# Mixture-of-experts stage: experts in order of their tokens, with rows by place and weights fetched by register

## What is computed

```python
def route(h2, w_router, router_bias):      # h2: (1088, 1024); 64 experts, each token takes 8
    s = sigmoid(h2 @ w_router); sb = s + router_bias
    ...                                     # best 4 of 8 groups by their two best scores, then top 8 of them
    w = s[idx] / sum(s[idx]) * 2.5
def routed_experts(h2, idx, wts, w_gate, w_up, w_down):
    xb = h2[toks]                           # tokens of expert e
    hb = silu(xb @ w_gate[e]) * (xb @ w_up[e])      # 1024 -> 256
    y = y.at[toks].add((hb @ w_down[e]) * ws[:, None])   # 256 -> 1024
```

## Time and profile before

| | us |
|---|---|
| median of 3 runs (2910.75 to 2916.51) | 2913.45 |
| the profiled execution | 2915.86 |
| its span, first to last instruction | 2914.1 |

### The profile page before, as it was taken

How to read it: one execution, slowest core, us unless ns; L and a number is a source line. 1 busy time by engine, 2 the same in 40 slices (tenths; PEclk the granted TensorE clock), 3 DMA queues, 4 the chain that set the end, 5 groups by cost and what they waited for, 6 DMA issues and landing times. The chain is left out here.

```text
span 2914.1 us, 43099 instructions
## 1 busy us (share of the span) xinstructions
PE 2641.9 (91%) x15610; PEld 2333.5 (80%) x15610; DVE 1934.3 (66%) x3001; ACT 1288.1 (44%) x1831; POOL 1491.7 (51%) x1668
## 2 busy tenths in 40 slices
PE   5999899898998989989869995999999999999991
PEld 5789698896978969789667654888888888888880
DVE  6474756647566475664776873777777777777764
ACT  3423424235252342523432312656666666666552
POOL 6455655646556465664652652454545444454530
PEclk9999999999999999999989997999999999999995
DMA  5101011110111101111034217899999999999966
GB/s 169 53 23 56 24 37 41 31 56 24 37 41 31 56 24 37 41 31 55 16 120 146 73 32 213 259 273 280 274 282 269 272 281 282 273 272 278 274 171 220
DMA packets 309592, 395.36 MB, mean 136 GB/s; under 512 B 22226, under 2 KB 260114, under 8 KB 309458
## 3 DMA queue, kind: packets, MB, share of 16 engines
q1 hardware_dynamic: 277250, 303.05, 31.9%
q0 software_dynamic: 30976, 86.09, 12.3%
q10 hardware_dynamic: 1232, 4.46, 0.6%
HBM read 324.15 MB, written 84.07 MB: 140 GB/s over the span
## 5 line engine op out<-in xcount | busy, mean ns | idle before, releaser
L113 PE MATMUL ps<-xTh,w_mix_low 128*128 128x368 f32 (+1 forms) x1728 | 594.2, 344 | 1.4 <-DVE xTl L107 1.4
L114 PE MATMUL ps<-xTl,w_mix_high 128*128 128x368 f32 (+1 forms) x1728 | 570.7, 330 | 0.0
L115 PE MATMUL ps<-xTh,w_mix_high 128*128 128x368 f32 (+1 forms) x1728 | 569.1, 329 | 0.0
L113 PEld LDWEIGHTS ps<-xTh,w_mix_low 128*128 128x128 f32 x1728 | 327.5, 190 | 10.6 <-issue 8.7
L114 PEld LDWEIGHTS ps<-xTl,w_mix_high 128*128 128x128 f32 x1728 | 327.6, 190 | 8.4 <-issue 7.0
L115 PEld LDWEIGHTS ps<-xTh,w_mix_high 128*128 128x128 f32 x1728 | 326.8, 189 | 0.0
L2028 PE MATMUL ps<-xghl,wgh 128*128 128x384 f32 x1024 | 298.9, 361 | 7.1 <-DVE xghl L107 7.1
L2028 PE MATMUL ps<-xghl,wuh 128*128 128x384 f32 x1024 | 296.1, 359 | 0.0
L1971 POOL DMA_INDIRECT ys_d<-yo,back x128 | 254.1, 1985 | 76.4 <-POOL back L1967 48.3
L2030 PE MATMUL ps<-xghl,wgl 128*128 128x192 f32 x1024 | 258.2, 252 | 0.0
L2030 PE MATMUL ps<-xghl,wul 128*128 128x192 f32 x1024 | 256.6, 251 | 0.0
(11 more groups left out here) (348 smaller groups left out, 6217.6 us busy)
## 6 DMA issues: line engine op xcount, KB each, us to landing
wg<-in_w_exp_gate SPq DMA_DIRECT2D x64, 1024.0 KB, 8.5
wu<-in_w_exp_up SPq DMA_DIRECT2D x64, 1024.0 KB
wd<-in_w_exp_down SPq DMA_DIRECT2D x64, 1024.0 KB
w_mix_raw<-in_w_in SPq DMA_DIRECT2D x72, 512.0 KB, 3.8
mT_d<-gs_m SPq DMA_DIRECT2D x8, 544.0 KB, 2.7
xr_m<-in_x_prompt SPq DMA_DIRECT2D x8, 512.0 KB, 3.6
xn_d<-xr_m SPq DMA_DIRECT2D x8, 512.0 KB, 3.1
out<-vrow_m SPq DMA_DIRECT2D x8, 512.0 KB, 4.8
```

The lines of the kernel that those rows point to most:

```text
L113: pe.matmul(out, ll, rh, start=start, stop=False)
L114: pe.matmul(out, lh, rl, start=False, stop=False)
L115: return pe.matmul(out, lh, rh, start=False, stop=stop)
```

## The change

Experts are no longer taken by number. `ranks` in the bridge compares the counts of all experts; experts 0 and 1 keep places 0 and 1 (`STATIC`), and the others follow by falling number of tokens. `order` holds the expert of each place and `place` is the matrix of the permutation. Each place has its own number of rows: 192 for places 0 to 3, 176 to place 9, 160 to 27, 152 to 39, 144 to 49, and 128 for the last 14, 152.5 on average. Places with 128 rows have a single tile: one gather, 8 transposes, 12 down products, two copies, one scatter-add. The list in DRAM keeps its 192 entries per expert by number; when `experts` reads it, it is multiplied by `place` where it was transposed before, which brings it into the new order. SyncE reads the expert's number of a place into a register (`value_load`) before the gate load; up and down loads use the same register. All loops over the experts are written out on every engine. `blocks` gets the room of each expert's place (`room`) instead of 192 and now waits for `order_out`; a table `limit_d` goes to DRAM for `overflow`, whose `late_slots` uses it. All of `rows_out` is on ScalarE. In the mixer a mask that equalled `before` is no longer built a second time.

The core of the diff:

```diff
+STATIC = 2
+RANK_CAPS = [(4, 192), (10, 176), (28, 160), (40, 152), (50, 144), (NE, 128)]
+PLACE_CAP = [next(cap for end, cap in RANK_CAPS if r < end) for r in range(NE)]
...
-            CONSTANTS = 4 + 3 * NL + 2
+            CONSTANTS = 3 + 3 * NL + 2
...
-                sp.wait_ge(kept, 16 * 9)
+                sp.dma_start(limit_d[:, :], limit[:, :]).then_inc(kept, 16)
+                sp.wait_ge(kept, 16 * 10)
...
+                    pe.matmul(ps[:NE, RB, NE:NE + 1], acc[:, t % 2, :], ones[:, 0:1], start=True, stop=False)
+                    pe.matmul(ps[:NE, RB, NE:NE + 1], chosen[:DEC, t, :], ones[:DEC, 0:1], start=False, stop=True).then_inc(cnt_done, 1)
+
+                def order_out():
+
+                    pe.wait_ge(ranked, 1)
+                    pe.matmul(ps[0:1, RB, 2 * NE:3 * NE], rowf[:NE, 0:1], place[:NE, :], start=True, stop=True)
+                    pe.matmul(ps[:, RB, 3 * NE:4 * NE], ones[:NE, :], fewer[:NE, :], start=True, stop=True).then_inc(ordered, 1)
...
-                for t in range(5, NT):
+                shared(5)
+                order_out()
+                for t in range(6, NT):
                     shared(t)
...
-                def rows_out(t):
-                    m = rows(t)
-                    dve.wait_ge(d_done, 2 * t + 2)
-                    if t < 2:
-                        dve.wait_ge(spare_out, 32)
-                    if t >= 2:
-                        dve.wait_ge(y_out[t % 2], 16 * (t // 2))
-                    dve.tensor_copy(ys[:m, t % 2, cols(1)], ps[:m, U, :]).then_inc(y_right, 1)
+                def ranks():
+                    for out, number in ((tie, NUM), (tie_col, rowf[:, 0:1])):
+                        ch(dve.tensor_scalar(out[:, :], number, -1.0, float(STATIC), ALU.mult, ALU.add))
+                        ch(dve.tensor_scalar(out[:, :], out[:, :], 0.0, float(NE * 2 * SEQ), ALU.max, ALU.mult))
+                        ch(dve.tensor_tensor(out[:, :], out[:, :], number, ALU.subtract))
+                    dve.wait_ge(cnt_done, 1)
+                    ch(dve.scalar_tensor_tensor(out=key[:, :], in0=ps[:, RB, 0:NE], scalar=float(NE), in1=tie[:, :], op0=ALU.mult,
+                                                op1=ALU.add))
+                    ch(dve.scalar_tensor_tensor(out=key_col[:NE, :], in0=ps[:NE, RB, NE:NE + 1], scalar=float(NE), in1=tie_col[:NE, :],
+                                                op0=ALU.mult, op1=ALU.add))
+                    ch(dve.tensor_scalar(more[:NE, :], key[:NE, :], key_col[:NE, 0:1], None, ALU.is_gt))
+                    ch(dve.tensor_reduce(place_col[:NE, :], more[:NE, :], AX.X, ALU.add))
+                    ch(dve.tensor_scalar(fewer[:NE, :], key[:NE, :], key_col[:NE, 0:1], None, ALU.is_lt))
+                    dve.tensor_scalar(place[:NE, :], NUM[:NE, :], place_col[:NE, 0:1], None, ALU.is_equal).then_inc(ranked, 1)
 
                 def blocks():
-                    dve.wait_ge(cnt_done, 1)
-                    ch(dve.tensor_scalar(cnt[:, 0, :], ps[:, RB, 0:NE], float(CAP), None, ALU.subtract))
-                    for k in range(7):
+                    dve.wait_ge(ordered, 1)
+                    ch(dve.tensor_copy(order[0:1, :], ps[0:1, RB, 2 * NE:3 * NE]))
+                    ends = [end for end, _ in RANK_CAPS]
+                    sizes = [cap for _, cap in RANK_CAPS]
+                    for n in range(len(sizes) - 1):
+                        ch(dve.tensor_scalar(cnt[:, 0, :], ps[:, RB, 3 * NE:4 * NE], float(ends[n]), float(sizes[n + 1] - sizes[n]), ALU.is_ge,
+                                             ALU.mult))
+                        if n == 0:
+                            ch(dve.tensor_scalar(room[:, :], cnt[:, 0, :], float(sizes[0]), None, ALU.add))
+                        else:
+                            ch(dve.tensor_tensor(room[:, :], room[:, :], cnt[:, 0, :], ALU.add))
+                    ch(dve.tensor_tensor(cnt[:, 0, :], ps[:, RB, 0:NE], room[:, :], ALU.subtract))
...
+                ranks()
                 hidden(5)
                 blocks()
-                for t in range(5, NT):
-                    rows_out(t)
...
-                    if t < 5:
-                        act.wait_ge(d_done, 2 * t + 2)
-                        act.activation(ys[:m, t % 2, cols(1)], ps[:m, U, :], ACT.Copy).then_inc(y_right, 1)
+                    act.wait_ge(d_done, 2 * t + 2)
+                    act.activation(ys[:m, t % 2, cols(1)], ps[:m, U, :], ACT.Copy).then_inc(y_right, 1)
...
+    second = [cap - P for cap in PLACE_CAP]
+    tiles = [1 + (n > 0) for n in second]
+    upto = [sum(tiles[:e]) for e in range(NE + 1)]
+    of_buffer = [[sum(tiles[r] for r in range(b, e, 2)) for e in range(NE + 1)] for b in range(2)]
...
-            def every_expert(eng, body):
-
-
-
-                def one(e):
-                    body(e, e % 2, lambda d: (e + d) // 2)
-                for e in range(5):
-                    one(e)
-                with eng.Fori(3, NE // 2 - 1) as j:
-                    for r in range(2):
-                        body(2 * j + r - 1, 1 - r, lambda d: j + (r - 1 + d) // 2)
-                for e in range(NE - 3, NE):
...
+            def transposed(e):
+
+                cap, c2 = PLACE_CAP[e], second[e]
+                out = [(xhl[:, :, 0:P], xhl[:, :, cap:cap + P], ps[:, TB:TB + 2, :].rearrange("p b (k n) -> p (b k) n", n=P))]
+                if c2:
+                    out.append((xhl[:, :, P:cap], xhl[:, :, cap + P:2 * cap],
+                                ps[:, TB + 2, 0:KT * c2].rearrange("p (k n) -> p k n", n=c2)))
+                return out
+
+            def row_tiles(e):
+                return ((0, P), (1, second[e]))[:tiles[e]]
...
+                names = ("w_exp_gate", "w_exp_up", "w_exp_down")
+                expert = {e: e for e in range(STATIC)}
+
+                def load(which, e):
+                    arrived, raw = ((g_in, wg), (u_in, wu), (d_in, wd))[which]
+                    if e not in expert:
+                        expert[e] = sp.value_load(order[0:1, e:e + 1], min_val=0, max_val=NE - 1)
+                    sp.dma_start(raw[:, e % 2, :, :], source(names[which], expert[e])).then_inc(arrived[e % 2], 16)
...
+                for e in range(NE):
+                    if e + 2 < NE:
                         for which in (GATE, UP):
                             sp.wait_ge(low[which], e + 1)
-                            load(which, e + 2, b)
-                    if at_least(e, 1) and at_most(e, NE - 2):
+                            load(which, e + 2)
+                    if 1 <= e < NE - 1:
                         sp.wait_ge(low[DOWN], e)
-                        load(DOWN, e + 1, 1 - b)
-                every_expert(sp, body)
+                        load(DOWN, e + 1)
...
+                def gather(e):
+                    b = e % 2
+                    if e >= 2:
+                        pool.wait_ge(x_in[b], 16 * of_buffer[b][e])
                         pool.wait_ge(t_done, e - 1)
-                    pool.tensor_copy(idx[:, b, 0:1], tab[:, bass.ds(e, 1), 0]).then_inc(idx_ready, 1)
-                    pool.tensor_copy(idx[:C2, b, 1:2], tab[:C2, bass.ds(e, 1), 1]).then_inc(idx_ready, 1)
-                    pool.wait_ge(idx_ready, 2)
-                    pool.sem_clear(idx_ready)
-                    for j, m in ((0, P), (1, C2)):
+                    indices(idx, idx_ready, e, 0)
+                    pool.wait_ge(idx_ready, upto[e + 1])
...
+                def turn(e):
+                    b, c2 = e % 2, second[e]
+                    pe.wait_ge(x_in[b], 16 * of_buffer[b][e + 1])
+                    if e:
+                        pe.wait_ge(x_low, upto[e])
                     for k in range(KT):
-                        pe.transpose(ps[:, TB + k // 4, k % 4 * P:(k % 4 + 1) * P], xg[:, b, 0, k * P:(k + 1) * P], ident[:, :])
-                    for k in range(KT):
-                        mm = pe.transpose(ps[:, TB + 2, k * C2:(k + 1) * C2], xg[:C2, b, 1, k * P:(k + 1) * P], ident[:C2, :C2])
+                        mm = pe.transpose(ps[:, TB + k // 4, k % 4 * P:(k % 4 + 1) * P], xg[:, b, 0, k * P:(k + 1) * P], ident[:, :])
+                    if c2:
+                        for k in range(KT):
+                            mm = pe.transpose(ps[:, TB + 2, k * c2:(k + 1) * c2], xg[:c2, b, 1, k * P:(k + 1) * P], ident[:c2, :c2])
                     mm.then_inc(t_done, 1)
 
-                def down(e, b, following):
+                def gate_up(e):
+                    cap = PLACE_CAP[e]
+                    pe.wait_ge(x_low, upto[e + 1])
+                    for which, wh, wl, bank, done in ((GATE, wgh, wgl, GB, g_done), (UP, wuh, wul, UB, u_done)):
+                        pe.wait_ge(low[which], e + 1)
+                        for f in range(2):
+                            if bank + f:
+                                wait_copied(e - 2, DB.index(bank + f))
+                            elif e:
```

(43 more changed lines are left out.)

263 lines of the change are left out of this document (116 added, 147 removed).

## The result

| | before | after |
|---|---|---|
| median of 4 runs, us | 2914.33 (2910.75 to 2916.51) | 2816.65 (2811.42 to 2820.84) |
| the profiled execution, us | 2915.86 | 2820.84 |
| its span, us | 2914.1 | 2819.1 |

The changed kernel takes 0.9665 of the time before (95% interval 0.9646 to 0.9684), 97.7 us less. Predicted were 2812 us, 2780 to 2848. The profiled execution is the slowest of the four.

A forecast was written before the change was run, and what follows sets the result against it. TensorE was taken to bound the experts, with transfers and vector work hidden under it. 99 us from smaller places plus 3 from the tail, 102 in all, gave 2813.9 or 2811.5 us; forecast 2812, range 2780 to 2848.

The forecast's parts named there:

- The bound and the pair: In `experts` TensorE sets the pace; a gate/up pair takes 177 + 108 = 285 ns, falling 0.83 ns per row cut.
- The transposes: Second group of eight per expert: 0.6 ns per column, winning 0.08 to 0.23 us; bounds 0 and twice that.
- The last 14 places: Places 50 to 63: VectorE's chain gives 12.7 us, transfers 12.6; taken as 12.9 us per place, bounds 11.2 and 14.0.
- Loops unrolled, register: Expert loops and weight loads: code fetching taken as 0; SyncE's register read 0, bounds 0 and 1 us once.
- The bridge: Ahead of the experts: `ranks` hidden, `blocks` ahead only of its own stores; taken as 0, bounds -2 and +4 us.
- my bound of 4: Stated sign of being wrong: the bridge moving by over 4 us.
- The tail: Last place adds one tile instead of two, saving a scatter issue and copies: -3 us (0 to -4).
- 1: Rival, gate/up pairs: no load floor, so the 192-column product shrinks too, 34 us more won, 2778 us; chance 0.10.
- 2, TensorE's pace: Rival: the last 14 places run at 11.2 us each, 24 us more won, 2788 us; chance 0.10.
- 3, transfers at 275 GB/s: Rival: transfers set the experts' pace at their average rate; 38 us won, 2874 us; chance 0.07.
- 4: Rival: code fetching in the unrolled loops stops TensorE, +55 us, 2867 us; chance 0.08.
- 5: Rival: an expert overflows its place's rows and the `If` is taken, +160 us, 2970 us; chance 0.03.

The follow-up runs named there:

- Run 1: The kernel before, with the low-weight product (line 2030) streaming 128 columns instead of 192: 2915.83 us, ratio 1.0003.
- run 7: The changed kernel without the scatter-adds of the last 14 places: 2806.47 us, ratio 0.9632.
- run 2: The changed kernel with 192 rows in every place, keeping order, register and unrolled loops: 2912.25 us, ratio 0.9994.
- run 5: The changed kernel measured once more, unedited, as partner on the same chip: 2810.86 us, ratio 0.9641.
- run 12: The kernel before without its store of the block list (63 rows of 4 bytes): 2912.35 us, ratio 0.9996.
- run 10: run 6's kernel without the store of the block list (67 rows of 4 bytes): 2797.30 us, ratio 0.9601.
- run 6: The changed kernel with VectorE making the low part of the next x right after the sums, ahead of three steps on h: 2803.28 us, ratio 0.9617.
- runs 9 and 10: The first is run 6's kernel without the block list and three more `overflow` tables: 2796.39 us, ratio 0.9595; the second is under run 10.
- run 11: run 6's kernel with the block list turned into one row and stored as one piece: 2802.28 us, ratio 0.9612.
- runs 6 and 8: The second is run 6's edit plus run 7's edit on the changed kernel: 2800.84 us, ratio 0.9613.
- runs 2 to 10: Those without own line: the changed kernel with 144 rows in the last 14 places, 2847.90 us; with two `overflow` tables stored as one row, 2813.43 us.

## Why the prediction was right

**The bound and the pair: right.** The distances between pairs are, as medians by place, 0.285, 0.272, 0.256, 0.251, 0.243 and 0.232 us; predicted 0.272, 0.258, 0.252, 0.245, 0.232. Two loads from TensorE's timeline of after, at 160 rows:

```profile
2106.30 0.19 PEld L2026 LDWEIGHTS ps<-xghl,wgh 128*128 128x128 f32 x1
2106.41 0.19 PEld L2028 LDWEIGHTS ps<-xghl,wgl 128*128 128x128 f32 x1
2106.56 0.19 PEld L2026 LDWEIGHTS ps<-xghl,wgh 128*128 128x128 f32 x1
```

The first distance is 0.11 still, the second fell from 0.18 to 0.15. Run 1 shows the same from the other side. The issue-gap formula of the Trainium skill ("TensorE: Matmul & The Clock Gate", Back-to-back issue gap) gives 0.165 us for a pair at 128 rows, as an estimate from 384 columns; the trace has 0.232. That section of the Trainium skill calls the formula the gap of an isolated product, which counts too little for narrow ones, as it has no budget for the loads; this case agrees.

**The transposes: the mis-sized term.** I took 0.08 to 0.23 us per expert from 0.6 ns per column. At 160 rows the eight second transposes are these:

```profile
2112.79 1.03 PE L2008 MATMUL ps<-ident,xg 128*128 128x128 f32 x8
2113.76 0.68 PE L2011 MATMUL ps<-ident,xg 32*128 32x32 f32 x8
2114.36 0.49 PE L120 MATMUL ps<-wdh,hTl 128*128 128x512 f32 x1
```

From 2113.76 to 2114.36 are 0.60 us, against 0.64 with 64 columns; the starts of such transposes lie 0.065 apart on average with 16 columns and 0.069 with 64. The lower bound, nothing, was nearly right. With that the steps from place 3 to place 49 fell by 46.0 us (from 750.7 to 704.7) where my list has 51.3, 7.8 of them for the transposes, which gave about 1.4 (0.64 us fell to 0.62, 0.61, 0.605 and 0.59). No step there is off by more than 0.22.

**The last 14 places: the right bound, a little too dear.** I put the chain at 5.3 us after the up products and the step at 12.9 because two limits lay near each other. The parts measure 0.7 late, 2.83, 1.22: 4.82, and the step 12.27. Taking 0.2 more than the chain's 12.7 for transfers of the same size was wrong: these places move at a share of 1.06 and 340 GB/s, above the 320 of the earlier trace rows, and nothing waits for them (run 7). The last 14 steps took 174.5 us instead of 228.5: 54.0 won where I had 47.9. Eleven of them are near 12.27; the first two, in which TensorE still has a second tile's work, are 13.87 and 13.77, and the last is 11.77. TensorE's wait is 1.1 us each, as this view of waits shows for 2590 to 2740 us; I had said about 1.4:

```profile
PE ps L2026 <- DVE xghl L114: 11.9, 12, 1.1
```

These two misses, 5 us too much and 6 too little, cancel: 100.2 won against 99.1 reckoned. The sum is better than its terms.

**Loops unrolled, register: right at nothing.** Code packets rose from 81 to 123 and TensorE has no idle time by them: run 2 in the time, and in after 70.00 us busy of 70 in the stretch that answers to the earlier trace rows.

```profile
1830.00:1900.00 70.00, 70.00 (x452) 61.38 (x451) 53.07 (x58) 43.77 (x50) 36.14 (x32) 1.00 0.91 263
```

**The bridge: the right size for the wrong reason.** I took 0 (-2 to +4), with `blocks` off the path since only the stores of its results hang on it. But those stores hang in front of the stage: they were late enough to lie just ahead of the last store of the shared expert, which then lands late, and the queue waits for all of them before the token list. That costs 7 us (11.5 instead of 4.3 in run 5). Before, the list lay beside an earlier store, and ScalarE waited 7.56 us there. So a cost moved and grew, from 4.9 us (run 12 against before) to 7.8 (run 10 against run 6), and the rest of the changed bridge won about 3 back, by single profiles; by which part isn't tested. The bridge is 245.7 us in run 5 and 246.4 before: that the two sides cancel so nearly is luck. The 251.8 of after's profiled execution, 5.4 more and so beyond my bound of 4, which I had named as a sign of being wrong, have the stall of unknown origin on top. `ranks` costs nothing that shows in these lengths.

**The tail: right in kind, too small.** One scatter is left for the last place, issued at 2756.86; the end after the last silu is 5.3 us shorter in these two executions, and I had 3, 4 at most.

**The rivals.** 1 fell by run 1 and the pair distances. 2, TensorE's pace, fell with the waits, though run 6 goes nearly half of the way from 12.27 to 11.2. 3, transfers at 275 GB/s, fell: 286 on average, 340 at the end. 4 fell by run 2. 5 didn't come: no blocks were taken.

**A version that beats both** is run 6: 2803.28 us, ratio 0.9617 (0.9601 to 0.9632), 7.6 us below after on the same chip. The block list as a row adds nothing that could be measured; without the list (runs 9 and 10) another 5 to 6 us are gone by the ratios, but their intervals overlap with that of run 6, so the profiles show this gain and the times don't. Storing it at another time, where nothing waits behind it, wasn't tried.

## What to carry to other kernels

Before rows are cut, measure the distances between weight loads: only the product that outlasts its load gets cheaper, the others and small transposes do not. Where a stretch looks bound by two resources at once, take each away alone; a DMA share of 1.06 was no bound here, and the order of seven short vector steps was. A store that nobody on the path reads can still hold up the next stage, by making the store beside it land late, and the name of the wait need not be the store that is to blame. Before a gain of 2 or 3 us is put down to an edit, compare the granted clock of the stretch in both profiles.

## What the runs showed of the hardware that was not expected

- 67 pieces of 4 bytes, one from each partition, issued 0.8 us ahead of a store of `ys`: that store lands 10.4 us after its issue, and 3.0 without them (runs 6 and 10). As one row, issued beside the store, the gap to the load behind it is 5.4 us instead of 11.8 (run 11).
- The 16 DMA engines moved 340 to 344 GB/s at a share of 1.06 and 1.07, and neither TensorE nor VectorE waited for a transfer; 296 GB/s gave the same step (runs 5 to 7).
- A product under a 128-column load costs the load, 0.108 us, with 192, 160 or 128 columns; small transposes start 0.065 to 0.069 us apart on average with 16 to 64 columns.
- The same wait of TensorE, 3.05 us in the first step, was followed by 6.8 us at the lower clock in runs 9 to 11 and by none in runs 6 and 8.
- A stall of about 5 us on ScalarE, with VectorE's steps standing still in part of it, appears in some executions and not in others of nearly the same kernel (after and run 11, not runs 2 to 10). Its cause is open.
